# Forgetting attention: the four forget rows stand beside the high parts of a head in tiles of 128 rows, contracted by the first score pass

## The reference, cut to what matters

```python
def block(args):                       # one block of 128 queries of _fox_attention
    qi, fi, bi = args
    q_pos = bi * Q_BLOCK + jnp.arange(Q_BLOCK)
    logits = jnp.einsum('bhqd,bhkd->bhqk', qi, k) * scale + (fi[..., :, None] - cum_f[..., None, :])
    logits = jnp.where(k_pos[None, :] <= q_pos[:, None], logits, -jnp.inf)
    p = jax.nn.softmax(logits, axis=-1)
    return jnp.einsum('bhqk,bhkd->bhqd', p, v)
```

## Time and profile before

| | |
|---|---|
| median of 3 runs | 4099.19 us (4090.66 to 4112.65) |
| the profiled execution | 4099.46 us |
| its span, first to last instruction | 4096.5 us |
| mean granted TensorE clock | 0.967 |
| PE busy | 3840.3 us (94%), 17196 matmuls |
| PEld busy | 3035.6 us (74%) |
| DVE busy | 1941.2 us (47%) |
| ACT busy | 1495.4 us (37%) |
| POOL busy | 381.8 us (9%) |
| chain that ended last | PE 73%, DVE 8%, ACT 7%, issue 6% |
| L1179, the four-row pass | 64 matmuls, 322 to 498 ns each |

### The profile page before, as it was taken

How to read it: one execution, slowest core, us unless ns; L and a number is a source line. 1 busy time by engine, 2 the same in 40 slices (tenths; PEclk the granted TensorE clock), 3 DMA queues, 4 the chain that set the end, 5 groups by cost and what they waited for, 6 DMA issues and landing times.

```text
span 4096.5 us, 48273 instructions
## 1 busy us (share of the span) xinstructions
PE 3840.3 (94%) x17196; PEld 3035.6 (74%) x17196; DVE 1941.2 (47%) x3222; ACT 1495.4 (37%) x2459; POOL 381.8 (9%) x332
## 2 busy tenths in 40 slices
PE   8999997799999999987899998899999999899999
PEld 6887664578888887665688887787777777677887
DVE  4433457654334423567554334335544444645652
ACT  3222343432223223333332234425634554533221
POOL 0100001101001101011101021011100000100110
PEclk9999998899999999997899999999999999999999
DMA  4333221033323333211033334131122113222332
GB/s 119 94 96 113 69 59 47 10 90 97 97 92 94 96 97 115 59 44 40 24 99 95 108 100 112 37 89 47 47 63 71 47 47 95 75 82 87 94 96 97
DMA packets 484450, 321.93 MB, mean 79 GB/s; under 512 B 10928, under 2 KB 464176, under 8 KB 483280
## 3 DMA queue, kind: packets, MB, share of 16 engines
q1 hardware_dynamic: 479616, 301.81, 25.3%
q0 software_dynamic: 3536, 16.13, 1.2%
q10 hardware_dynamic: 1152, 2.10, 0.1%
HBM read 310.82 MB, written 8.52 MB: 78 GB/s over the span
## 4 chain that ended last, share of the span: by engine, by line
PE 73%; DVE 8%; ACT 7%; issue 6%; DVEq 4%; DMA 1%; POOLq 0%; ACTq 0%; POOL 0%; SPq 0%
PE bank L235 21%; PE bank L237 20%; PE bank L236 20%; ACT w_hi L220 2%; DVE w_lo L227 1%; PE bank L1191 1%; DVEq L2509 1%; PE bank L1202 1%; PE bank L1194 1%; PE bank L2206 1%; PE bank L1193 1%; PE bank L1175 1%; PE bank L977 1%; DVEq L1016 1%; DVE s_ring L2514 1%
## 5 line engine op out<-in xcount | busy, mean ns | idle before, releaser
L235 PE MATMUL bank<-h_hi,w_hi 128*128 128x512 f32 x3064 | 1231.4, 402 | 67.9 <-DVE h_lo L389 25.1
L227 DVE TENSOR_TENSOR w_lo<-w_raw,w_hi 128x1024 fp32r<-128x1024 f32 (+1 forms) x571 | 742.5, 1302 | 1036.2 <-ACT w_hi L220 1033.0
L237 PE MATMUL bank<-h_lo,w_hi 128*128 128x512 f32 x3128 | 1230.6, 393 | 0.0
L236 PE MATMUL bank<-h_hi,w_lo 128*128 128x512 f32 x3064 | 1204.6, 393 | 0.0
L220 ACT ACTIVATE w_hi<-w_raw 128x1024 fp32r<-128x1024 f32 (+1 forms) x571 | 591.5, 1038 | 622.1 <-DMA w_raw<-in_ffn_w_down 315.7
L235 PEld LDWEIGHTS bank<-h_hi,w_hi 128*128 128x128 f32 x3064 | 579.5, 189 | 235.1 <-issue 100.0
L237 PEld LDWEIGHTS bank<-h_lo,w_hi 128*128 128x128 f32 x3128 | 591.3, 189 | 131.1 <-issue 2.0
L236 PEld LDWEIGHTS bank<-h_hi,w_lo 128*128 128x128 f32 x3064 | 580.0, 189 | 114.7 <-issue 2.2
L235 PE MATMUL bank<-g_hi,w_hi 128*128 (+1 forms) x880 | 342.4, 389 | 2.3 <-DVE gu_ring L2525 2.3
L236 PE MATMUL bank<-g_hi,w_lo 128*128 (+1 forms) x880 | 342.3, 389 | 0.0
L237 PE MATMUL bank<-g_lo,w_hi 128*128 (+1 forms) x880 | 342.3, 389 | 0.0
(11 more groups left out here) (452 smaller groups left out, 4605.0 us busy)
## 6 DMA issues: line engine op xcount, KB each, us to landing
w_raw<-in_w_in SPq DMA_DIRECT2D x105, 512.0 KB, 3.8
w_raw<-in_ffn_w_gate SPq DMA_DIRECT2D x88, 512.0 KB, 3.8
w_raw<-in_ffn_w_up SPq DMA_DIRECT2D x88, 512.0 KB, 3.8
w_raw<-in_ffn_w_down SPq DMA_DIRECT2D x88, 512.0 KB, 3.4
w_raw<-in_w_mix SPq DMA_DIRECT2D x50, 512.0 KB, 3.9
w_raw<-in_w_up SPq DMA_DIRECT2D x44, 512.0 KB, 3.7
w_raw<-in_w_branch SPq DMA_DIRECT2D x32, 512.0 KB, 3.9
w_raw<-in_w_down SPq DMA_DIRECT2D x22, 512.0 KB, 3.2
```

Source lines behind the costliest of these rows:

```text
L227: dve.tensor_tensor(WL[:, slot(c), 0:w], RAW[:, slot(c), 0:w], WH[:, slot(c), 0:w].bitcast(F32), ALU.subtract).then_inc(w_lo, 1)
L235: pe.matmul(bank, wh, xh, start=start, stop=False)
L236: pe.matmul(bank, wl, xh, start=False, stop=False)
L237: return pe.matmul(bank, wh, xl, start=False, stop=stop)
```

## The change

The score step loses its fourth pass. The high parts of q and k move out of `QH` and `KH` to new tiles `FQH` and `FKH` of 128 partitions, with two slots and, in each slot, one plane per half: a head's 64 features stand in their old partitions, its four forget rows in the first four partitions of the other half, and the rest is zero. The first pass contracts all 128 rows (`whole`), the two others 64 as before.

Around this: ACT and POOL split q and k in two pieces of 64 rows each instead of one of 128, with a drain on POOL after each piece (the condition also holds for one pair group of block 1 per layer). DVE sets both tiles to zero and then the rows that hold ones, with drains between. ACT waits for those memsets (`ff_set`) before the first splits, and POOL before its first DMAs, which now stand ahead of its first splits. The rows are loaded pair by pair, four DMAs a pair, two pairs at the start and one more after each pair's low part of k, once the steps that read the slot are done. PE waits for a pair's rows at its first step.

```diff
@@ attend_pe_parts
                 if n % 8 == 0:
                     pe.wait_ge(sp_lo, s0 + (3 * (n // 8) + 2))
+                    if x["whole"]:
+                        pe.wait_ge(fq_in[n // 8 % 2], 64 * (n // 16 + 1))
+                        pass_wait(pe)
                 pe.wait_ge(smax_done, n0 + (n + 1))
                 bank = at.scores(n, x["width"])
-                pe.matmul(bank, x["q"][0], x["k"][0], start=True, stop=False)
+                pe.matmul(bank, *(x["whole"] or (x["q"][0], x["k"][0])), start=True, stop=False)
                 pe.matmul(bank, x["q"][0], x["k"][1], start=False, stop=False)
-                last = pe.matmul(bank, x["q"][1], x["k"][0], start=False, stop=not x["extra"])
-                if x["extra"]:
-                    last = pe.matmul(bank, *x["extra"], start=False, stop=True)
-                last.then_inc(qk_done, 1)
+                pe.matmul(bank, x["q"][1], x["k"][0], start=False, stop=True).then_inc(qk_done, 1)
@@ split_pool
         for raw, hi_, lo_ in jobs[j]:
             last = pool.tensor_tensor(lo_, raw, hi_.bitcast(F32), ALU.subtract)
+            if len(jobs[j]) > 1 and hi_.shape[0] < P:
+                pool.drain()
@@ tiles
-    FQ = g("forget_q", 48, [P, 4, S], F32R)
-    FK = g("forget_k", 56, [P, 4, S], F32R)
+    FQH = g("forget_q_hi", 48, [P, 2, 2, S], F32R)
+    FKH = g("forget_k_hi", 56, [P, 2, 2, S], F32R)
@@ fox_steps, fox_jobs
+            fox_steps += head_steps((FQH[rows, g_ % 2, half, :], FXQL[rows, g_ % 4, :]),
+                                    (FKH[rows, g_ % 2, half, :], FXKL[rows, g_ % 4, :]), half, causal_mask, g_, 3,
+                                    whole=(FQH[:, g_ % 2, half, :], FKH[:, g_ % 2, half, :]))
+        fox_jobs += [[(FXQ[half_rows(b), g_ % 4, :], FQH[half_rows(b), g_ % 2, b, :], FXQL[half_rows(b), g_ % 4, :])
+                      for b in range(2)],
+                     [(FXK[half_rows(b), g_ % 4, :], FKH[half_rows(b), g_ % 2, b, :], FXKL[half_rows(b), g_ % 4, :])
+                      for b in range(2)], v_job(FXV[:, g_ % 4, :, :])]
@@ block2_act
         act.wait_ge(hv_done, HF + 1)
+        act.wait_ge(ff_set, 2)
+        pass_wait(act)
         for j in range(3):
             split_act(act, fox_jobs, j, JF, fox_ready(j))
@@ block2_dve
-        dve.memset(FQ[:, :, :].bitcast(F32), 1.0).then_inc(ff_set, 1)
-        dve.memset(FK[:, :, :].bitcast(F32), 1.0).then_inc(ff_set, 1)
+        for tile in (FQH, FKH):
+            dve.memset(tile[:, :, :, :].bitcast(F32), 0.0)
+            dve.drain()
+            dve.memset(tile[64:68, :, 0, :].bitcast(F32), 1.0)
+            dve.memset(tile[0:4, :, 1, :].bitcast(F32), 1.0).then_inc(ff_set, 1)
+        dve.drain()
         dve.wait_ge(ff_st, 64)
@@ block2_pool
+    def forget_rows(pool, pair):
+        if pair >= 2:
+            pool.wait_ge(qk_done, SF + 8 * (pair - 1))
+            pass_wait(pool)
+        slot_ = pair % 2
+        for half, at_ in ((0, 64), (1, 0)):
+            h = 2 * pair + half
+            pool.dma_start(FQH[at_:at_ + 2, slot_, half, :], dram_f[0:2, h, :]).then_inc(fq_in[slot_], 16)
+            pool.dma_start(FKH[at_ + 2:at_ + 4, slot_, half, :], dram_f[2:4, h, :]).then_inc(fq_in[slot_], 16)
...
         pool.wait_ge(ff_st, 64)
-        for j in range(3):
+        pool.wait_ge(ff_set, 2)
+        pass_wait(pool)
+        forget_rows(pool, 0)
+        forget_rows(pool, 1)
+        for j in range(len(fox_jobs)):
             split_pool(pool, fox_jobs, j, JF)
-        pool.wait_ge(ff_set, 2)
-        for a in range(4):
-            for c in range(4):
-                pool.dma_start((FQ, FK)[a // 2][a:P:32, c, :], dram_f[a, 4 * c:4 * c + 4, :]).then_inc(fq_in, 16)
-        for j in range(3, len(fox_jobs)):
-            split_pool(pool, fox_jobs, j, JF)
+            pair = j // 3
+            if j % 3 == 1 and 1 <= pair and pair + 1 < 8:
+                forget_rows(pool, pair + 1)
```

More of the change, by code:

```diff
@@ L1025, in step, with head_steps @@
         return dict(i=i, width=width, qk=qk, mask=mask, v=v, out=out, group=group, kts=width // P)
-    def head_steps(q, k, half, mask, group, bank, extra=None):
+    def head_steps(q, k, half, mask, group, bank, whole=None):
         steps = []
@@ L1033, in head_steps @@
             steps.append(dict(i=i, width=w, q=(q[0][:, cols], q[1][:, cols]), k=(k[0][:, 0:w], k[1][:, 0:w]),
-                              extra=extra and (extra[0][:, cols], extra[1][:, 0:w]), mask=mask(i, w), half=half,
+                              whole=whole and (whole[0][:, cols], whole[1][:, 0:w]), mask=mask(i, w), half=half,
                               group=group, bank=bank))
@@ L1747, in build @@
     ff_set = sem("forget_ones_set")
-    fq_in = sem("forget_in")
+    fq_in = [sem(f"forget_in_{k}") for k in range(2)]
     z_done = sem("sb_scores")
@@ L1985, in build @@
                  for h in range(4) for i in range(TT)]
-    def fox_extra(tile):
-        return lambda h: tile[32 * (h % 4):32 * (h % 4) + 4, h // 4, :]
     def in_pair(tile, h):
@@ L2760, in fox_hook @@
                 e.wait_ge(mx_done, KT + 2)
-                e.wait_ge(fq_in, 256)
         woven(FOX_STEPS_AND_TAIL, 3 * (len(fox_items1) + 2),
```

## The result

The changed kernel takes 4104.36 us (median of 12 runs, 4099.66 to 4107.95), the kernel before beside it 4096.54 us (12 runs, 4090.24 to 4112.65): a ratio of 1.002, with a 95% interval of 1.0011 to 1.003. So it is slower, by about 8 us (4.5 to 12), where I had forecast 6 us less. 4104 lies inside the range of 4080 to 4106; the sign is wrong. The profiled execution took 4107.73 us, its span 4105.9.

What follows compares the result with a forecast made beforehand. PE was taken to bound the forgetting attention (busy 271.9 of 277.9 us). Terms: −15.7 on PE, +9.1 for the seam, +0.6 for block 1's drains, −6.0 in all, so 4093 us, range 4080 to 4106.

Steps and rivals of the forecast that it cites:

- The saving on PE: Score steps of the forgetting attention: dropping the fourth pass saves PE 21.1 us over 64 steps, less 2.9 for costlier entries.
- Rival B: Score steps: nothing gained on PE while the seam is paid, 4109 us; chance 0.08.
- the 128-row entry: First score pass: with 128 rows like the projection ahead, it starts after 0.23 us instead of 0.32.
- I give 2.5 us to that and to ACT's later bank copies: Forgetting attention: 2.5 us of PE's saving lost to longer waits where PE waited anyhow and to ACT's later copies.
- save where PE waits for ACT's bank copy: ACT's two extra pieces per pair, 1.1 us in 35: hidden, except PE's waits for bank copies, counted in the 2.5.
- The seam: Before the "mem" branch: ACT waits for DVE's memsets, PE stands 6.7 us, clock loses 2.4; costs 9.1 (3.5 to 10.5).
- rival A: Seam hidden, costing 3.5 us or less, if four-partition memsets are cheaper and the clock holds; 4087 us; chance 0.2.
- POOL's splits: Attention pair starts: k's low part 3.3 us later against 3.6 slack; perhaps 0 to 1 us waiting at the last.
- Rival C: Pair starts: late POOL pieces make PE wait 1.5 us at each of 7 pairs, 10 us; 4103 us; chance 0.07.
- Block 1's drains: Block 1, first layer: three POOL drains ahead of k's semaphore lengthen PE's wait, +0.6 us (0 to 1.2).
- The sum: Whole kernel: −15.7 + 9.1 + 0.6 = −6.0 us against the profiled 4099.46; 4093 us predicted.

Runs made afterwards that it cites:

- kernel 8: The kernel before without its fourth pass, forget term left out, splits, memsets and loads as before: 4083.06 us, ratio 0.9973.
- kernel 3: The changed kernel with ACT's second high piece of q and k left out, POOL's pieces kept: 4095.77 us, ratio 0.9997.
- kernel 7: Kernel 6 with POOL instead of ACT making the second high pieces of q and k: 4086.84 us, ratio 0.9981.
- kernel 1: The changed kernel with the six memsets made early by POOL instead of by DVE at the seam: 4093.28 us, ratio 0.999.
- kernel 2: The changed kernel without POOL's drains in block 1, those in the forgetting attention kept: 4100.20 us, ratio 1.0.
- kernel 5: The kernel before with only the four POOL drains per layer in block 1's split added: 4098.55 us, ratio 1.0008.
- kernel 4: The kernel before, fourth pass kept, with q and k split in two 64-row pieces on ACT and POOL, with drains: 4104.27 us, ratio 1.0014.
- kernel 6: The changed kernel with the memsets made early by POOL and without the drains in block 1: 4089.64 us, ratio 0.9986.

## Why the prediction was wrong, step by step

**The saving on PE: right.** Forecast 21.1 less 2.9, 18.2 us of work; measured 19.2 in the changed kernel and 19.5 with the pass simply gone. Rival B (nothing gained) falls with it: the 128-row entry costs 0.23.

**The failing step: "I give 2.5 us to that and to ACT's later bank copies".** It was 10.2 us (idle 6.0 to 16.2). With that number in place of the 2.5 the forecast of −6.0 becomes +1.7, so this term alone turns the sign. By the runs it has two parts:

- *5.3 us, PE faster by itself* (kernel 8: 6.0 to 11.3). The step's end shows why. The changed kernel, PE, ACT and DVE at the last step of a head:

```profile
2872.14 0.62 ACT L1219 ACTIVATE probs<-probs,minus_row_max 128x384 f32<-128x384 f32 x1 [2.06 <-DVE minus_row_max L1261]
...
2872.47 0.40 PE L1180 MATMUL bank<-forget_k_hi,forget_q_hi 128*128 128x512 f32 x1
...
2872.75 0.57 ACT L1226 ACTIVATE turned_hi<-bank 128x512 fp32r<-128x512 f32 x1
...
2873.36 0.69 DVE L1275 TENSOR_TENSOR turned_lo<-bank,turned_hi 128x512 fp32r<-128x512 f32 x1 [0.75 <-ACT turned_hi L1226]
...
2874.10 0.50 PE L1193 MATMUL bank<-turned_hi,pair_v_hi 128*128 128x512 f32 x1 [0.58 <-DVE turned_lo L1275]
```

and the kernel before at the same step:

```profile
2860.49 0.58 ACT L1224 ACTIVATE turned_hi<-bank 128x512 fp32r<-128x512 f32 x1
2860.64 0.50 PE L1175 MATMUL bank<-pair_k_hi,pair_q_hi 64*128 64x512 f32 x1
...
2861.10 0.69 DVE L1273 TENSOR_TENSOR turned_lo<-bank,turned_hi 128x512 fp32r<-128x512 f32 x1 [0.76 <-ACT turned_hi L1224]
...
2861.54 0.50 PE L1179 MATMUL bank<-forget_k,forget_q 4*128 4x512 f32 x1
2861.96 0.50 PE L1191 MATMUL bank<-turned_hi,pair_v_hi 128*128 128x512 f32 x1
```

The product behind the fourth pass needs turned_lo. Before, turned_lo ended at 2861.79 and the product began at 2861.96: 0.17 us of slack, and PE worked through. After, it ended at 2874.05, and PE stood 0.58 us ahead of 2874.10. From ACT's turned_hi to the product it is 1.47 us before and 1.35 after: ACT and DVE set the pace here, and the 0.42 us taken from PE's step bought 0.12. Everything needed stood in the trace of before; I read only waits that were there, not those 0.2 us from being there. Eight such waits and one at L1204 make up 6.3 us against 2.0.

- *4.9 us, ACT's extra pieces* (kernel 8 has 11.3 idle, the changed kernel 16.2; kernel 3, which has the change's POOL work but not these, has 11.5). I had counted 1.1 us per pair on ACT as hidden "save where PE waits for ACT's bank copy". In the changed kernel ACT's timeline at a pair:

```profile
2855.17 1.26 ACT L1133 ACTIVATE forget_k_hi<-pair_k 64x512 fp32r<-64x512 f32 x2
2856.45 1.06 ACT L220 ACTIVATE w_hi<-w_raw 128x1024 fp32r<-128x1024 f32 x1
2857.54 1.72 DVE L227 TENSOR_TENSOR w_lo<-w_raw,w_hi 128x1024 fp32r<-128x1024 f32 x1 [1.55 <-ACT w_hi L220]
2859.19 0.73 DVE L886 SCALAR_TENSOR_TENSOR pair_q<-pair_q,block_vectors,bank 128x512 f32<-128x512 f32 x1
2860.02 0.60 ACT L854 ACTIVATE t_ring<-bank 128x512 f32<-128x512 f32 x1 [2.51 <-DVE pair_q L886]
...
2860.76 0.47 PE L235 MATMUL bank<-h_hi,w_hi 128*128 128x512 f32 x1 [1.10 <-ACT t_ring L854]
```

One chain through four engines, each next one idle until the last is done: the two pieces 1.26 instead of 0.62, then w_hi, then DVE's w_lo and pair_q, then t_ring, then PE, 1.1 us late. From ACT's split of k to its t_ring it is 3.81 us in the kernel before (2843.36 to 2847.17) and 4.85 here. Most of the 1.04 is ACT's extra piece; 0.26 is DVE's w_lo, 1.46 before and 1.72 here, which starts while POOL makes its low parts (kernel 7). ACT is busy 60% of the stage and it still goes straight to PE, six times.

**The seam: right.** 9.1 us forecast, 8.9 measured in the profiles and 11.1 by the medians of kernel 1. The last memset ended at 2677.80, 8.66 us after the first began (forecast 8.7); the splits, the table and the weight unit followed as said:

```profile
2669.14 1.76 DVE L2685 MEMSET forget_q_hi<- 128x2048 f32 x1 [0.38 <-issue]
2671.21 0.91 DVE L2687 MEMSET forget_q_hi<- 4x1024 f32 x1 [0.31 <-issue]
...
2676.89 0.91 DVE L2688 MEMSET forget_k_hi<- 4x1024 f32 x1 [0.25 <-issue]
2678.00 1.27 ACT L1133 ACTIVATE forget_q_hi<-pair_q 64x512 fp32r<-64x512 f32 x2 [10.07 <-DVE forget_k_hi L2688]
...
2681.23 1.28 ACT L2055 ACT_TABLE_LOAD   x1
2682.53 1.06 ACT L220 ACTIVATE w_hi<-w_raw 128x1024 fp32r<-128x1024 f32 x1
...
2684.89 0.79 PE L235 MATMUL bank<-branch_hi,w_hi 128*128 128x512 f32 x1 [7.16 <-DVE w_lo L227]
```

PE stood 7.2 us (forecast 6.7), and the clock after it was at its lower level, 0.51 of full speed, for 3.4 us, 1.7 us lost (forecast 5.3 and 2.4), as the view by windows shows:

```profile
2684.80:2688.20 3.40, 3.31 (x8) 2.63 (x9) 3.10 (x3) 2.77 (x4) 3.24 (x2) 0.51 0.00 0
```

So rival A falls. A memset of 1024 elements on four partitions took 0.91, as the elements had said.

**POOL's splits: right, and closer than I liked.** The last pair's, answering to the earlier trace rows:

```profile
2992.82 1.29 POOL L1140 TENSOR_TENSOR pair_q_lo<-pair_q,forget_q_hi 64x512 fp32r<-64x512 f32 x1 [0.48 <-issue]
2994.27 3.53 POOL L1140 TENSOR_TENSOR pair_k_lo<-pair_k,forget_k_hi 64x512 fp32r<-64x512 f32 x2 [0.16 <-issue]
```

They end at 2997.80; that pair's first score starts at 2997.94, and PE never waits for POOL in the stage. Rival C falls in its place (POOL), though its kind was right: gain turned to waits, on ACT and DVE instead.

**Block 1's drains: too low, and no fixed price.** Forecast 0.6 (at most 1.2). Kernels 2 and 5 put them at 4.2 and 3.5 us by medians, and the interval of kernel 5 reaches down to nothing. The profiles show why no single number comes out. Kernel 3 has the drains and matches the kernel before up to them, within 0.4 us and with the same changes of clock. There PE's wait for k's low part grew from 1.3 to 1.7 us, and 1.3 us later the granted clock fell to its lower level, 0.50, where the kernel before kept 1.00 (timeline of PE, and view by windows):

```profile
750.96 0.33 PE L1180 MATMUL bank<-two_k_hi,two_q_hi 96*128 96x128 f32 x1 [1.72 <-POOL b_k_lo L1140]
752.30:755.70 3.40, 3.40 (x11) 2.63 (x10) 2.05 (x7) 1.51 (x6) 0.00 (x0) 0.50 0.00 0
```

Its block 1 is 3.5 us longer. Kernels 2 (without drains) and 5 (with them) reach this place with other changes of clock behind them; both take 132.1 us at a mean clock of 0.82, so there no cost of the drains shows. Kernel 7, without drains, took 136.6 at 0.75. The forecast counted the drains' own time and not what the clock does after a longer wait. Why the executions differ in their clock ahead of that place stays open.

**The sum.** With the measured terms: −19.2 work, +10.2 idle, +8.9 seam, +1.5 to 3.5 in block 1: +1.4 to +3.4 us. The medians say +7.8 (4.5 to 12), so 4 to 6 us of the median lie in no stage that the change touches, and the sum stays just under the interval. Part of it may be scatter: at POOL's first split of block 1's split group (745.57 us before, 752.08 after) the two profiled executions already stand 6.5 us apart, though both kernels are the same up to there. Kernels 4 and 6 came out 4.1 and 3.5 us above what their stages say (+6.6 against +2.5, −5.4 against −8.9), kernels 5 and 8 about 2 above, kernels 1, 2 and 3 within 1.1, and kernel 7 about 3 below. That rest is open.

## What to carry to other kernels

Before counting work taken from the bound engine as time saved, look behind each removed instruction at when its follower's other inputs are ready: here a slack of 0.17 us bounded a saving of 0.42, and no table of waits showed it, since nobody waited yet. Removing the work outright, with the result left incomplete, prices the whole prize in one run: 12 us here, out of which an 8.9 us seam had to be paid. An idle engine is the place for one-time preparation (POOL here), not the queue of one that feeds the bound engine. It is not free where it runs beside DVE, though: see kernel 7. And "55% busy" hides nothing where the engine is one link of a chain that runs straight to PE.

## What the runs showed of the hardware that I had not expected

- After a stand of 7.2 us the clock was low for 3.4 us; after one of 5.5 it was low for 5.3. The longer stand did not cost more. In both the clock had fallen within the stand, at 2681.2 and at 3592.4 us; the longer stand had more of the low stretch in it (3.6 us at 0.51, against 1.5).
- The same code can take 130.6, 132.1 or 136.6 us in block 1 (kernels 6, 2 and 7), at mean granted clocks of 0.86, 0.82 and 0.75.
- DVE's split of 128x1024 took at most 1.23 us when it started with POOL at rest, in all ten profiles, and up to 2.28 in the attention of the changed kernel when it started while POOL made a low part.
- The same memset of 2048 elements takes 1.76 us on DVE and 1.81 on POOL; that of 1024, 0.91 and 0.94.
